# Rotary halves exchanged by DMA instead of by a matmul, and one weight split behind the value banks' copies

## The reference, cut to what matters

```python
def apply_axial_rope(x, cos, sin):
    xr = x.reshape(*x.shape[:-1], 2, ROPE_AXIS_DIM)     # two axes of 32 features
    x1, x2 = jnp.split(xr, 2, axis=-1)                  # 16 and 16
    rot = jnp.concatenate([-x2, x1], axis=-1)
    return (xr * c + rot * s).reshape(x.shape)
```

## Time and profile before

| what | value |
|---|---|
| median of three executions | 1785.63 us |
| the profiled execution's own time | 1787.35 us |
| its span, first to last instruction | 1785.6 us |
| PE busy | 1611.1 us (90%), 11038 matmuls |
| DVE busy | 898.4 us (50%) |
| ACT busy | 722.1 us (40%) |
| POOL busy | 168.2 us (9%) |
| mean granted TensorE clock | 0.946 of 2.4 GHz |
| HBM read | 443.83 MB |

### The profile page before, as it was taken

One profiled execution on the slowest core, in us unless ns is written; L12 is line 12 of the kernel. 1 busy time (PEld: TensorE's weight loads), 2 busy tenths in 40 slices (PEclk: granted clock), 3 DMA queues, 4 the chain that ended last, 5 costly groups with the idle time before them and its releaser, 6 DMA issues.

```text
span 1785.6 us, 26627 instructions
## 1 busy us (share of the span) xinstructions
PE 1611.1 (90%) x11038; PEld 1328.8 (74%) x11038; DVE 898.4 (50%) x1104; ACT 722.1 (40%) x936; POOL 168.2 (9%) x82
## 2 busy tenths in 40 slices
PE   6999985767676689999998999999999999999998
PEld 4877742323232358999997999989999899998886
DVE  4765210101010158566585765686656657566665
ACT  4434220101010155445335544464445665355443
POOL 0200000000000002111001111111111001111110
PEclk9999897878787889999899999999999999999999
DMA  9568999999999986555541555556555555455551
GB/s 366 182 231 315 406 427 427 427 429 428 429 427 428 426 294 198 189 183 174 179 156 65 187 184 188 181 189 204 186 190 193 197 183 172 151 183 179 196 186 62
DMA packets 181648, 446.18 MB, mean 250 GB/s; under 512 B 8022, under 2 KB 139471, under 8 KB 163127
## 3 DMA queue, kind: packets, MB, share of 16 engines
q1 hardware_dynamic: 178080, 437.84, 66.3%
q10 hardware_dynamic: 3062, 4.98, 0.8%
q0 software_dynamic: 416, 2.10, 0.3%
HBM read 443.83 MB, written 1.06 MB: 249 GB/s over the span
## 4 chain that ended last, share of the span: by engine, by line
PE 72%; DMA 17%; DVE 6%; ACT 2%; issue 1%; SPq 0%; POOL 0%; DVEq 0%; ACTq 0%
PE wk L838 16%; PE wk L841 8%; DMA arena<-in_w_up_dram 8%; PE wk L1320 8%; PE acc L810 5%; PE acc L811 5%; PE acc L812 5%; DMA ex_ring<-in_w_up_dram 4%; PE wk L810 3%; DMA ring<-in_w_up_dram 3%; PE wk L811 3%; PE wk L812 3%; DVE w_lo L593 2%; PE wk L890 2%; PE wk L891 2%
## 5 line engine op out<-in xcount | busy, mean ns | idle before, releaser
L593 DVE TENSOR_TENSOR w_lo<-ring,w_hi 128x2048 fp32r<-128x2048 f32 x198 | 452.7, 2289 | 189.2 <-ACT w_hi L584 188.5
L584 ACT ACTIVATE w_hi<-ring 128x2048 fp32r<-128x2048 f32 x198 | 377.4, 1907 | 236.1 <-PE acc L812 97.8
L838 PE MATMUL wk<-h_both,w_hi 128*128 128x512 f32 x1344 | 336.9, 392 | 2.3 <-DVE gated L2609 1.3
L838 PEld LDWEIGHTS wk<-h_both,w_hi 128*128 128x128 f32 x1344 | 242.3, 189 | 47.5 <-issue 2.5
L2165 POOL TENSOR_TENSOR hid_lo<-gated,hid_hi 128x512 fp32r<-128x512 f32 x44 | 124.8, 2836 | 1123.5 <-ACT hid_hi L1972 1123.5
L810 PE MATMUL acc<-hid_hi,w_hi 128*128 128x256 f32 x720 | 204.7, 284 | 1.4 <-DVE arena L2825 0.8
L811 PE MATMUL acc<-hid_lo,w_hi 128*128 128x256 f32 x720 | 203.7, 283 | 0.0
L812 PE MATMUL acc<-hid_hi,w_lo 128*128 128x256 f32 x720 | 203.7, 283 | 0.0
L841 PEld LDWEIGHTS wk<-h_both,w_lo 128*128 128x128 f32 x1344 | 183.4, 190 | 13.1
L841 PE MATMUL wk<-h_both,w_lo 128*128 128x256 f32 x1344 | 187.4, 282 | 0.0
L1320 PE MATMUL wk<-ex_ring,arena 128*32 128x512 f32 x400 | 112.3, 750 | 64.6 <-DMA arena<-in_w_up_dram 64.6
(11 more groups left out here) (431 smaller groups left out, 2791.5 us busy)
## 6 DMA issues: line engine op xcount, KB each, us to landing
ring<-in_ffn_w_in_dram SPq DMA_DIRECT2D x88, 1024.0 KB, 5.1
ring<-in_ffn_w_out_dram SPq DMA_DIRECT2D x44, 1024.0 KB, 4.9
ring<-in_w_ada_dram SPq DMA_DIRECT2D x24, 1024.0 KB, 6.7
ring<-in_b_w_in_dram SPq DMA_DIRECT2D x24, 1024.0 KB, 5.2
ex_ring<-in_w_up_dram SPq DMA_DIRECT2D x9, 2048.0 KB, 15.6
ex_ring<-in_w_down_dram SPq DMA_DIRECT2D x9, 2048.0 KB, 24.2
ex_ring<-in_w_gate_dram SPq DMA_DIRECT2D x9, 2048.0 KB, 24.6
ring<-in_w_gate_dram SPq DMA_DIRECT2D x8, 2048.0 KB, 24.4
```

Source lines behind the costliest of these rows:

```text
L584: nc.scalar.activation(w_hi[:, v % SPLIT, 0:n], ring[:, u % RING, 0:n], ACT.Copy).then_inc(w_hi_ready, 1)
L593: eng.tensor_tensor(w_lo[:, v % SPLIT, 0:n], ring[:, u % RING, 0:n], w_hi[:, v % SPLIT, 0:n].bitcast(F32), ALU.subtract).then_inc(w_lo_rea ...
L838: mm(banks[:, m, :], wh[:, k, f], h_both[:, k, :, :], start=k == 0, stop=False, skip_group_check=True)
```

## The change

There are three edits.

The `rotate` matmuls are gone. In their place ScalarE issues transfers from SBUF to SBUF (`swap_halves`): eight for the query and eight for the key, each of 16 partitions and 4 KB per partition, straight into `qT` and `kT`. The eight for the query stand ahead of the copies of the third and fourth token group, the eight for the key behind them and ahead of the copy of the spread table. The sign is in the sine table now. VectorE's `rope` waits for the transfers and multiplies `qT` and `kT` in place of the PSUM bank. The waits that `rotate` held stay on TensorE: those for `std_ready` and `reldist_sb` now stand ahead of the first context group, the one for `lame_ready` behind the second.

```diff
-            def rotate(r):
-                pe.wait_ge(grp_out, r + 1)
-                if r == 0:
-                    pe.wait_ge(std_ready, 2)
-                elif r == 1:
-                    pe.wait_ge(reldist_sb, 1)
-                elif r == 2:
-                    pe.wait_ge(lame_ready, 1)
-                mm(accf[:, r * 512:(r + 1) * 512], rot, raw[:, 2 * r:2 * r + 2, :].rearrange("p k t -> p (k t)"),
-                   start=True, stop=True).then_inc(rope_ps, 1)
+            pe.wait_ge(std_ready, 2)
+            pe.wait_ge(reldist_sb, 1)
             hc = (hc_hi, hc_lo)
             pe.wait_ge(h_scaled, 2 * KT)
             for a in range(2, 4):
                 group(lambda b: project3(b, split_of(U_IN + a), src=hc), ends_unit=True)
-                rotate(2 * a - 4)
-                rotate(2 * a - 3)
+                if a == 3:
+                    pe.wait_ge(lame_ready, 1)
...
+            def swap_halves(dst, src, done, ready):
+                act.wait_ge(grp_out, done)
+                for lo in range(0, P, 16):
+                    to = lo + 16 if lo % 32 == 0 else lo - 16
+                    act.dma_start(dst[to:to + 16, :, :], src[lo:lo + 16, :, :]).then_inc(ready, 16)
...
             A(lam_exp, accf[:, 1024:1026], ACT.Exp).then_inc(lame_ready, 1)
+            swap_halves(qT, raw[:, 0:4, :], 2, rope_in)
             for j in range(2):
                 take(half(raw[:, 4 + 2 * j:6 + 2 * j, :]))
+            swap_halves(kT[:, :, CTX:CTX + T], raw[:, 4:8, :], 4, rows_in)
             act.wait_ge(rel_ps, 1)
             A(reldist[:, :], accf[0:HEADS2, 512:1024], ACT.Copy).then_inc(reldist_sb, 1)
...
-                dve.wait_ge(rope_ps, r + 1)
+                if r < 2:
+                    dve.wait_ge(rope_in, 128)
+                else:
+                    dve.wait_ge(rows_in, 16 * N_ROWS + 128)
                 dve.wait_ge(rope_cos, r + 1)
-                link(V.tensor_tensor(tmp, accf[:, r * 512:(r + 1) * 512].rearrange("p (k t) -> p k t", k=2),
-                                     sinT.rearrange("p (o t) -> p o t", o=1).to_broadcast([P, 2, T]), ALU.mult))
                 dst = qT[:, 2 * r:2 * r + 2, :] if r < 2 else kT[:, 2 * r - 4:2 * r - 2, CTX:CTX + T]
+                link(V.tensor_tensor(tmp, dst, sinT.rearrange("p (o t) -> p o t", o=1).to_broadcast([P, 2, T]), ALU.mult))
```

```diff
             split_high(VA + 11)
+            split_high(VA + 12)
             for pair in range(2):
-                split_high(VA + 12 + 2 * pair)
                 for t in range(TT):
                     A(vA[:, t, pair * 512:(pair + 1) * 512], bank(U_A + 12 + 2 * pair), ACT.Copy,
                       scale=rstd[:, T + t:T + t + 1]).then_inc(grp_out, 1)
-                if pair == 0:
-                    split_high(VA + 13)
+                split_high(VA + 13 + pair)
```

More of the change, by code:

```diff
@@ L125, in constants @@
     put("cos", np.cos(ang.astype(np.float64)))
-    put("sin", np.sin(ang.astype(np.float64)))
+    put("sin", np.sin(ang.astype(np.float64)) * np.where(p % 32 < 16, -1.0, 1.0)[:, None])
     n = np.outer(tok, tok) % T
@@ L298, in build @@
         grp_ps, grp_out = sem("grp_ps"), sem("grp_out")
-        rope_ps, rope_cos, rope_done = sem("rope_ps"), sem("rope_cos"), sem("rope_done")
+        rope_in, rope_cos, rope_done = sem("rope_in"), sem("rope_cos"), sem("rope_done")
         sc_ps, max_ready, exp_ready, attn_ready = (sem("sc_ps"), sem("max_ready"), sem("exp_ready"),
@@ L2324, in rope @@
             def rope(r):
-                dve.wait_ge(rope_ps, r + 1)
-                dve.wait_ge(rope_cos, r + 1)
-                dve.wait_ge(rope_ps, r + 1)
+                if r < 2:
+                    dve.wait_ge(rope_in, 128)
+                else:
+                    dve.wait_ge(rows_in, 16 * N_ROWS + 128)
                 dve.wait_ge(rope_cos, r + 1)
                 tmp = ropea[:, r % 2, :, :]
-                link(V.tensor_tensor(tmp, accf[:, r * 512:(r + 1) * 512].rearrange("p (k t) -> p k t", k=2),
-                                     sinT.rearrange("p (o t) -> p o t", o=1).to_broadcast([P, 2, T]), ALU.mult))
                 dst = qT[:, 2 * r:2 * r + 2, :] if r < 2 else kT[:, 2 * r - 4:2 * r - 2, CTX:CTX + T]
+                link(V.tensor_tensor(tmp, dst, sinT.rearrange("p (o t) -> p o t", o=1).to_broadcast([P, 2, T]), ALU.mult))
                 V.tensor_tensor(dst, tmp, ropeb[:, r % 2, :, :], ALU.add).then_inc(rope_done, 1)
```

## The result

The changed kernel takes 1792.64 us, median of 11 runs (1789.4 to 1794.7), against 1786.02 us of the kernel before (11 runs, 1784.6 to 1789.5) on the same chip. The ratio is 1.0031, 95% interval 1.0024 to 1.0039: slower by 0.3%, 6.6 us. The profiled execution took 1793.58 us with a span of 1791.7, so 6.1 us of span more than before.

The account below looks back on a forecast made before the run. TensorE bounds the first attention, and the transfer-bound experts' stage passes its time on. Terms -3.4 + 3.5 + 0.1 = +0.2 us on the median 1785.63 gave 1785.8 us, no change; range 1784.2 to 1789.4.

Parts of the forecast that it names:

- What bounds the kernel: First attention: TensorE bounds until 91.70, so its savings count whole; the transfer-bound experts' stage passes them on.
- The removed matmuls, -3.4: First attention, TensorE: four rotation matmuls of 512 columns go, saving 3.4 us, all of it counting.
- The moved wait, +3.5: Ahead of the first context group: TensorE stalls 3.5 us for ScalarE's spread-table copy behind issues of 0.39 us each.
- the long step: ScalarE's queue: upper bound of 0.62 us an issue; both batches count, 16 steps less 2.8, a 7.1 us stall, +3.7 us.
- The clock falls in the stall: Rival, first context group: TensorE's clock drops to half behind the new stall, costing 3.0 us, giving 1788.8; chance 0.10.
- The signs of being wrong: First context group starting near 63 or beyond 70, clock row of 0.50 behind the stall, or a rope awaiting a landing.
- Dear issues: Rival, ScalarE's queue ahead of the spread-table copy: slower from 0.61 us a step, or one 4.1 us issue; chance 0.12.
- Ropes and landings at nothing: First attention: ropes start at GpSimd's first product, about 66.5; the exchange's landings have slack and cost nothing.
- VectorE: First attention: VectorE runs 1.6 us late to the first maxima; its 2.60 us wait before the next maxima absorbs it.
- Attention A, +0.1: Attention A: scores start 1.8 us earlier, but VectorE's low split delays the maxima, +0.1 us; bounds -1.8 and +0.3.

Follow-up runs that it names:

- e14: Changed kernel with both exchanges issued by SyncE, GpSimd's cosine products first, VectorE's low split late, and the spread-table wait behind the first context group: 1781.02 us, ratio 0.9965.
- e12: Kernel before with seven kinds of transfers added behind ScalarE's last instruction, only to time issues: 0.61 to 0.62 us median within SBUF; kernel time not counted.
- e10: Changed kernel with the spread table ahead of the key's issues, GpSimd's cosine products ahead of its side transfers, and VectorE's low split behind attention A: 1783.36 us, ratio 0.9984.
- e7: Kernel before, rotation still by matmul, with GpSimd's cosine products ahead of its side transfers: 1785.87 us, ratio 1.0001.
- e16: Changed kernel with four of the key's eight transfers issued by SyncE in place of ScalarE: 1790.42 us, ratio 1.0018.
- e6: Changed kernel with TensorE's spread-table wait behind the first context group and GpSimd's cosine products ahead of its side transfers: 1786.09 us, ratio 1.0001.
- e13: Changed kernel with the spread table's copy ahead of the key's issues and GpSimd's cosine products ahead of its side transfers: 1784.58 us, ratio 0.9991.
- e1: Changed kernel with attention A's order put back, so the rotary edit alone: 1790.78 us, ratio 1.0023.
- e3: Changed kernel with TensorE's wait for the spread table's copy behind the first context group instead of ahead of it: 1789.18 us, ratio 1.0008.
- e5: Changed kernel with six filler matmuls in front of TensorE's wait for the spread table, to hold the clock: 1790.26 us, ratio 1.0020.
- e2: Kernel before with attention A's new order alone: 1785.79 us, ratio 0.9993.
- e8: Kernel before with attention A's new order and VectorE's low split put behind the attention: 1783.53 us, ratio 0.9989.
- e9: Changed kernel with ScalarE's copy and transfer of the spread table ahead of the key's eight issues: 1786.38 us, ratio 1.0002.

## Why the prediction was wrong, step by step

- *What bounds the kernel* held: TensorE up to the split at 91.70, later 97.00, and the experts' stage passed 5.3 us on as 5.0.
- *The removed matmuls, -3.4*: held; in e14's profile they give it in full.
- *The moved wait, +3.5*: this is the step that failed, by its size. The mechanism was named and found in its place: TensorE behind ScalarE's copy behind the issues. But the step "I take this, since the queue, the issuing engine and the sizes are nearest", 0.39 us, measured 0.68 in the key's batch and 0.61 in e12, at the far bound of 0.62 or beyond it. The nearest rows were of another kind, loads from main memory, which take 0.44 in e12; that both ends lay in SBUF outweighed queue and size. TensorE's group started 6.0 us late, 2.5 us more than forecast.
- The formula for the long step was wrong too, the other way: it let both batches count (16 steps less 2.8, 7.6 us at 0.65). The query's issues had started at 57.14, ahead of ScalarE's own work, and were hidden; only the key's counted. That was partly luck of the time: in e10 the same batch ended later than the fourth group and cost 0.7 us.
- *The clock falls in the stall* was a rival at 0.10 and 3.0 us. It came, and the profiles price it at 2.3 to 2.4 in the changed kernel. The row that I held against it, 3.15 us at 1.00 in attention A, was one row of one execution: e7 lost the clock behind the same wait. e16 lost it behind 3.65 us and e10 behind 1.38, while e6 kept it behind 1.33. The Trainium skill's rule ("TensorE: Matmul & The Clock Gate", section "Why this matters for your kernels") on idle gaps between bursts had it right for the stall, and the trace agrees: 0.50 behind the gap.
- The two went together, since a long step makes a long stall, and a long stall takes the clock. I gave them separate chances and let the range end at one of them: 1789.4. Together they are 1785.8 + 2.5 + 2.3 = 1790.6; with the 1.0 of attention A, 1791.6, and 1792.64 was measured. (I gave the range's lower end twice, as 1785.2 and as 1784.2; the miss is at the upper end.)
- *The signs of being wrong*: one of three came, the clock row of 0.50 behind the stall. The first context group started at 69.61, inside the 63 to 70 that I allowed, and no rope waited for a landing.
- *Dear issues* (0.12): right in its direction, but by the number of ordinary issues and not by one block of 4 us.
- *Ropes and landings at nothing*: in the changed kernel no rope waited for a landing, and the exchange landed in 2.4 to 3.1 us. In e6, e10 and e13, where the products are early, the first rope did wait, 1.2 us, and it cost nothing. But GpSimd's products, costed at the 65.25 of before, aren't there in time in every execution: side transfers stand ahead of them, and one of these was issued 5 to 7 us late in e1, e3, e5 and e16. The changed kernel's stall covers that; once the stall was gone, e3 paid 4.6 us and the clock behind it. The term was missing.
- *VectorE*: the wait of its second maxima for TensorE absorbed its own lateness, as forecast, but that lateness was 0.4 us and not 1.6 (2.23 left of 2.60); both maxima were late by the stall.
- *Attention A, +0.1*: held in its mechanism, that the low split takes the wait's place (third scores at the same distance, e2 no gain, 1.8 us in e8's profile when that split goes). Missing was 1.0 us of fallen clock, which e2's profile shows as well (1.4 us) without a loss in its median. The order doesn't decide it alone: the clock held in three profiles with it and fell in one without it.

## What to carry to other kernels

Price an issue by where both ends of its transfer lie, not by the queue that it is on, and count only the batch behind which the waiting engine stands. A wait placed behind a block of issues on another engine wants its signal sent ahead of that block: one reordering was worth 6.3 us here. When a stall is forecast on TensorE, price it with the clock behind it in the same case and not as a rival of its own; one profile in which the clock held behind such a wait is no proof, since the next execution can lose it. And look on every engine for small transfers that stand ahead of work that the new path needs.

## What the runs showed of the hardware that I had not expected

- An issue within SBUF cost its queue 0.61 to 0.62 us in the median for 4 KB to 128 KB on 1 to 32 partitions, and 0.57 for 256 KB on 64; from main memory 0.44 (e12), and from SBUF to main memory 0.29 (e9, one issue). Two queues that issued within SBUF at once took longer: 0.79 us an issue on both ScalarE's and SyncE's (e16).
- ScalarE's queue issues ahead of ScalarE's arithmetic: three transfers went out before and during the work up to 58.96, table load included (changed kernel).
- The clock was 0.50 behind idle gaps of 5.96 us (changed kernel), 4.6 (e3), 3.65 (e16) and 1.38 (e10), and 1.00 behind 1.33 (e6), 0.88 (e13) and 0.72 (e9). Behind the same 3.15 us in attention A it was 1.00 before and 0.50 in e7.
- GpSimd's issue of a small transfer came behind a gap of 6.7 us in e3, while 16-partition transfers were in flight; in the changed kernel that gap was 2.8.
